# One low half in four of the expert up-projections is made by POOL in two passes, not by DVE

## The reference, cut to what matters

```
s = sigmoid(x @ router_w)                 # 16 experts in 4 groups
# per token: the best group, in it the best 2 experts, weights normalised
out = swiglu(x, shared weights)
for e in range(16):
    out += gate[:, e] * ((silu(x @ wg[e]) * (x @ wu[e])) @ wd[e])
x = LN(alpha * x + out)
```

## Time and profile before

| | us |
|---|---|
| median of 3 runs (lowest, highest) | 1202.74 (1200.73, 1203.47) |
| the profiled execution | 1198.9 |
| its span, first to last instruction | 1197.1 |
| busy: PE, DVE, ACT, POOL | 1063.9, 851.2, 677.0, 79.9 |
| mean granted clock of TensorE | 0.956 of full speed |

### The profile page before, as it was taken

One profiled execution on the slowest core, in us unless ns is written; L12 is line 12 of the kernel. 1 busy time (PEld: TensorE's weight loads), 2 busy tenths in 40 slices (PEclk: granted clock), 3 DMA queues, 4 the chain that ended last, 5 costly groups with the idle time before them and its releaser, 6 DMA issues.

```text
span 1197.1 us, 24982 instructions
## 1 busy us (share of the span) xinstructions
PE 1063.9 (89%) x10266; PEld 810.9 (68%) x10266; DVE 851.2 (71%) x1454; ACT 677.0 (57%) x1067; POOL 79.9 (7%) x70
## 2 busy tenths in 40 slices
PE   6989999888996899999598999989889968999992
PEld 4767777666764699954267777766657647999441
DVE  4686566545876799988677765664559667999875
ACT  5645444544345678776567344544533466777654
POOL 0030000001003000000303000000010120000003
PEclk9989999999998899999889999999989979999996
DMA  9634333322432299987444434432225413899841
GB/s 358 230 121 129 128 128 97 123 72 88 141 126 87 80 312 323 321 296 293 176 147 172 146 112 141 129 114 89 90 74 166 129 55 135 315 337 330 310 159 46
DMA packets 59014, 204.35 MB, mean 171 GB/s; under 512 B 7016, under 2 KB 10244, under 8 KB 58376
## 3 DMA queue, kind: packets, MB, share of 16 engines
q1 hardware_dynamic: 54452, 192.85, 46.7%
q10 hardware_dynamic: 4436, 9.77, 2.3%
HBM read 199.19 MB, written 3.40 MB: 169 GB/s over the span
## 4 chain that ended last, share of the span: by engine, by line
PE 56%; DVE 20%; ACT 11%; DVEq 6%; issue 6%; DMA 1%; SPq 1%; ACTq 1%
PE bank L1548 33%; DVE wlo L925 8%; PE bank L1983 6%; ACT whi L466 5%; PE bank L1571 2%; DVEq L965 2%; PE bank L1910 2%; PE bank L1996 1%; PE bank L1900 1%; DVEq L1471 1%; PE bank L1680 1%; PE bank L1726 1%; PE bank L1675 1%; ACT acc L680 1%; DMA w<-in_w 1%
## 5 line engine op out<-in xcount | busy, mean ns | idle before, releaser
L925 DVE SCALAR_TENSOR_TENSOR wlo<-w,whi 128x1024 f16<-128x1024 f32 x360 | 446.9, 1264 | 126.5 <-ACT whi L466 125.4
L466 ACT ACTIVATE whi<-w 128x1024 f16<-128x1024 f32 x360 | 371.5, 1048 | 87.4 <-PE bank L1548 67.8
L1548 PE MATMUL bank<-xhi,whi 128*128 128x320 f16 x768 | 233.0, 303 | 7.6 <-DVE wlo L925 7.6
L1548 PE MATMUL bank<-xlo,whi 128*128 128x320 f16 x768 | 232.5, 303 | 0.0
L1548 PE MATMUL bank<-xhi,wlo 128*128 128x320 f16 x768 | 232.3, 302 | 0.0
L1548 PE MATMUL bank<-arena_b,whi 128*128 128x128 f16 x2048 | 179.2, 219 | 0.0
L1548 PE MATMUL bank<-arena_b,wlo 128*128 128x128 f16 x1024 | 175.2, 219 | 0.0
L1548 PEld LDWEIGHTS bank<-arena_b,whi 128*128 128x128 f16 x2048 | 157.1, 98 | 0.0
L1548 PEld LDWEIGHTS bank<-xhi,whi 128*128 128x128 f16 x768 | 76.4, 100 | 40.3 <-issue 9.2
L1548 PEld LDWEIGHTS bank<-arena_b,wlo 128*128 128x128 f16 x1024 | 100.2, 98 | 0.0
L1548 PEld LDWEIGHTS bank<-xhi,wlo 128*128 128x128 f16 x768 | 76.0, 99 | 30.6
(11 more groups left out here) (348 smaller groups left out, 1876.8 us busy)
## 6 DMA issues: line engine op xcount, KB each, us to landing
w<-in_w SPq DMA_DIRECT2D x360, 512.0 KB, 4.7
arena_b<-head_rows ACTq DMA_DIRECT2D x2, 1920.0 KB, 7.3
rows<-in_rows ACTq DMA_DIRECT2D x2, 1024.0 KB
xT<-in_x SPq DMA_DIRECT2D x2, 640.0 KB, 4.7
out_y<-xT SPq DMA_DIRECT2D x4, 320.0 KB
out_ckv<-arena_a ACTq DMA_DIRECT2D x2, 320.0 KB
c_init<-in_c_init ACTq DMA_DIRECT2D x2, 258.0 KB
out_c_prompt<-c_st ACTq DMA_DIRECT2D x8, 64.5 KB
```

Of the source, the lines that this page charges most:

```text
L466: A(whi[:, n % SLOTS, :], w32[:, n % RAW, :], ACT.Copy, scale=WS).then_inc(hi_done.sem, 1)
L925: V.scalar_tensor_tensor(wlo[:, n % SLOTS, :], w32[:, n % RAW, :], WS, whi[:, n % SLOTS, :], ALU.mult, ALU.subtract).then_inc(lo_done.sem, 1)
L1548: ins = M(out, w[:, s, sub * P:(sub + 1) * P], rhs(part, k), start=(n == 0), stop=(n == 3 * len(subs) - 1))
```

## The change

The fourth block of each of the 16 experts (not of the shared one) gets its low half from POOL, in two passes: w32 times 64, in place, then a drain, then minus whi, into wlo. This stands in POOL's program between the two norms and has a count of its own, lo_pool. DVE skips these blocks. lo_done now counts 16 fewer per layer, so waits on it are renumbered (lo_count), and SP and PE wait for the one or the other count, by block. ready_general serves the branch for groups of over 128 tokens, which isn't taken with these inputs.

```
+def by_pool(n):
+    return U0 + 4 <= n < D0 and (n - U0) % 4 == 3
+
+
+def lo_count(n):
+    layer, n = divmod(n, NB)
+    if by_pool(n):
+        return layer * EXPERTS + (n - U0) // 4
+    return layer * (NB - EXPERTS) + n + 1 - sum(by_pool(m) for m in range(n))
...
-        lo_done = sig("lo_done", NB)
+        lo_done = sig("lo_done", NB - EXPERTS)
+        lo_pool = sig("lo_pool", EXPERTS)
...
                 if n >= RAW:
-                    sp.wait_ge(lo_done.sem, n - RAW + 1)
+                    m = n - RAW
+                    sp.wait_ge((lo_pool if by_pool(m % NB) else lo_done).sem, lo_count(m))
                 load(n)
...
                 for k in range(2):
+                    if k:
+                        for e in range(EXPERTS):
+                            n = l * NB + U0 + 4 * e + 7
+                            pool.wait_ge(hi_done.sem, n + 1)
+                            G.tensor_scalar(w32[:, n % RAW, :], w32[:, n % RAW, :], WS, None, ALU.mult)
+                            pool.drain()
+                            G.tensor_tensor(wlo[:, n % SLOTS, :], w32[:, n % RAW, :],
+                                            whi[:, n % SLOTS, :], ALU.subtract).then_inc(lo_pool.sem, 1)
...
             def lo_at(l, n):
                 n += l * NB
-                if n < L * NB:
+                if n < L * NB and not by_pool(n % NB):
...
             def ready(l, n):
-                pe.wait_ge(lo_done.sem, lo_done.value(l, n + 1))
+                pe.wait_ge((lo_pool if by_pool(n) else lo_done).sem, lo_count(l * NB + n))
...
```

More of the change, by code:

```diff
@@ L1556, in ready, with ready_general, z_group @@
             def ready(l, n):
-                pe.wait_ge(lo_done.sem, lo_done.value(l, n + 1))
+                pe.wait_ge((lo_pool if by_pool(n) else lo_done).sem, lo_count(l * NB + n))
+            def ready_general(l, n, j=0):
+                if j == 3:
+                    pe.wait_ge(lo_pool.sem, lo_pool.value(l, n + 1))
+                else:
+                    pe.wait_ge(lo_done.sem, lo_done.value(l, n))
             def z_block(l, n, s, b):
                 ready(l, n)
+                z_group(s, b)
+            def z_group(s, b):
                 group(bank[b][:, 0:T], range(8), s, x_rhs).then_inc(blk_done.sem, 1)
@@ L1894, in down @@
                 def down(l, n, s, banks, expert, first, last):
-                    ready(l, n)
+                    ready_general(l, n + 1 - EXPERTS)
                     for kt in range(2):
@@ L2028, in _ @@
                                 pe.wait_ge(u_free.sem, u_free.value(l, e * 2 + (1 + j // 2)))
-                            z_block(l, g0 + j, (U0 + j) % SLOTS, UPB[j])
+                            ready_general(l, e if j == 3 else e * 3 + (U0 + 5 + j), j)
+                            z_group((U0 + j) % SLOTS, UPB[j])
                             if j == 0:
```

## The result

The changed kernel takes 1254.34 us (median of 4 runs, 1252.88 to 1256.34) against 1201.74 before: ratio 1.0439, 95% interval 1.0416 to 1.0463, that is +52.6 us. The profiled execution took 1254.7 us, 55.8 more than the one before. The forecast was slower, by 33 us.

A forecast was written before the change was run, and what follows sets the result against it. DVE was taken to bound the expert stage, with PE close behind. Mutually excluded work of 3 x 1.14 + 0.34 + 3.7 = 7.46 us against 6.44 per expert gave +32.6 us, 1235 by the median; range 1211 to 1266.

The forecast's parts named there:

- DVE sets the pace, PE is 0.14 us behind, so little can be won: Expert stage: DVE bounds each expert, PE is 0.14 to 0.16 us behind; freeing DVE gains at most 4.5 us.
- the PE case: Rival, expert stage: POOL's passes end inside the slack, PE's 6.14 us sets the pace; -4.5 us, 1198; chance 0.04.
- The second pass: POOL's subtraction of whi in the expert stage, taken at 2.4 us from neighbouring two-tensor rows.
- The drain: Between POOL's two passes in the expert stage, taken at 0.1 us.
- The first pass: POOL's product with 64 in the expert stage, taken at 1.2 us, near the memset's price.
- a dear first pass: Rival: POOL's product costs 2.4 us like a two-input one, T = 4.9; +71 us, 1274; chance 0.13.
- What has to wait for whom: Expert stage: POOL's passes and DVE's two-SBUF-operand operations exclude each other; their sum, 7.46 us, becomes the period, from 6.44.
- The latency: Expert stage: POOL has about 3.35 us before PE stands still; at T = 3.7 PE waits some 0.4 us.
- only the latency counts: Rival, expert stage: POOL and DVE don't hold each other, T passes the slack by 0.4; +8 us, 1211; chance 0.08.
- The buffers and DMA at no cost: Expert-stage loads: buffers come free some 3 us later, covered by over 12 us until next use; priced at nothing.
- No loss of clock: Expert stage: PE's share falls to 82%, a stretch 87% busy kept clock 1.00, so no loss counted.
- Where the time goes: Extra time falls in the expert stages, equal in both layers, period about 7.5 us; everything outside keeps its length.

The follow-up runs named there:

- The memset kernel: Changed kernel with both POOL passes replaced by three memsets of 2048 elements on spare memory, which read nothing: 1264.54 us, ratio 1.0531.
- the first experiment: Kernel before, DVE still making all four low halves, POOL running both passes beside it on spare memory with nobody waiting: 1263.14 us, ratio 1.0515.

## Why the prediction was right or wrong

*DVE sets the pace, PE is 0.14 us behind, so little can be won*: right for the first three groups. In the fourth, in both layers, the chain of the kernel before runs on PE alone, 6.14 us per expert (501.05 - 494.91 is the step from one gather to the next):

```profile
494.91 0.67 PE bank L1910 x12
...
501.05 0.67 PE bank L1910 x12
```

The kernel without the first pass won 0.23% (forecast of the PE case: 4.5 us, 0.4%); next behind DVE's work came not PE's 6.14 but the round of DVE and ACT, 6.27.

*The second pass*: 2.4 us taken, 2.13 alone and 2.46 with the wait for DVE. Right. *The drain*: 0.1 taken, 0.15.

*The first pass*: 1.2 us taken, 2.77 measured. This is the term that was mis-sized. It was put near the memset "as one stream is read and one written"; POOL's arithmetic doesn't go by the number of streams, as the copy (1.04) and the product by a constant (2.77) show. The rival "a dear first pass" (2.4 us) came nearest. The estimate of 0.9 us from the Trainium skill (GPSIMD Engine Reference, Engine selection: one-input work is roughly line rate) doesn't hold for this product; the copy, 1.04 us, is near it.

*What has to wait for whom*: the step that failed. The sum of what excludes each other, 3 x 1.14 + 0.34 + T, took T whole, but the product holds DVE only in its first 0.9 us. With measured numbers the sum is 3.76 + 0.9 + 2.13 = 6.8 us at most, and 5.9 where, as in the changed kernel, no low half starts early in a product. Either is under the 8.19 that came, so it wasn't the limit; with T whole it would be 3.76 + 5.42 = 9.2 us, more than that. DVE was held, as forecast (a low half of 3.15 us each turn), but it had time for it, since PE and ACT came round only every 8.19 us. One of the prediction's own signs of being wrong came, low halves at 1.2 us beside running passes, though only beside the first pass.

*The latency*: worked out in the prediction (3.35 us of slack) and then used only in the rival "only the latency counts". This is the limit that decides: at T = 5.42 that rival's own working (PE's 6.14, and what T and the signal have over the slack) gives 6.14 + 5.42 + 0.05 - 3.35 = 8.26 us, against 8.19. Its condition, that nothing holds anything, was not needed; the longer of the two limits rules. So the forecast of 1235 came from a limit that was too high for its T and a T that was too low: with the 3.7 us taken, the ring would have turned in 2.77 + 3.7 = 6.47 us and cost next to nothing. The two errors work against each other, and it is luck that the measured 1254 lies within 1211 to 1266. The memset kernel shows that the ring suffices.

*The buffers and DMA at no cost*: nothing in the trace speaks against it; the DMA share fell to 0.63. *No loss of clock*: wrong in a small part, 0.98 in the stretch of the earlier trace rows against 1.00, where PE was busy 78%, below the 82% that had been compared with 87%.

*Where the time goes*: right. The row of subtractions in the second layer's first norm starts at 991.70 instead of 963.31, 28.4 us later, half of the total before the second expert stage begins. The first line is of before, the second of after:

```profile
963.31 6.59 POOL L450 TENSOR_TENSOR acc<-acc,mu_var 128x320 f32<-128x320 f32 x7 [3.94 <-ACT mu_var L474]
991.70 6.58 POOL L473 TENSOR_TENSOR acc<-acc,mu_var 128x320 f32<-128x320 f32 x7 [3.94 <-ACT mu_var L497]
```

## What to carry to other kernels

When work moves to an idle engine, follow the buffer round: from the consumer that frees it, through every engine that refills it, back to the consumer. The new period is the longest of these rings, unless an engine's own work with what holds it is longer still, as in the first experiment; it is not the sum of busy times. And a slow helper belongs outside the ring (the same pass made ahead cost 9 us instead of 53). Price the helper's operation by one of the same kind, and where there is none, carry the dear end into the forecast.

## What the runs showed of the hardware

On POOL, a float32 product with a constant takes 2.77 us at 128x1024, a product with a repeated column 1.89, float32 minus float16 2.13, a copy 1.04. How long POOL holds DVE goes by the kind of operation. A two-tensor operation of POOL holds DVE's operations on two SBUF tensors almost to its end (3.15 us for 1.22). The product with a constant and the copy hold them only in their first 0.9 us (2.07 and 1.64 us for 1.22); later in the product they take 1.23. The product is itself stretched by them, to 3.56 and 3.72 us from 2.77. Why the one-input operations behave so was not tried.
